# V of a head pair as 512-column products for three of five token chunks, in a fused mLSTM and retention step

## What is computed

```python
def retention_mixer(u, w_in, decay_exp, g_norm, w_out, S0, grid):
    z = jnp.einsum('btd,de->bte', u, w_in).astype(F32)
    hk, hv = B_HEADS * B_DK, B_HEADS * B_DV
    q, k, v, gate = jnp.split(z, [hk, 2 * hk, 2 * hk + hv], axis=-1)
    ...
    v = v.reshape(B, T, B_HEADS, B_DV).transpose(0, 2, 1, 3)
    ...
    h_f, S_f = retention_scan(q, k, v, log_gamma[0], S0[:, 0])
    h_b, S_b = retention_scan(flip_t(q), flip_t(k), flip_t(v), log_gamma[1], S0[:, 1])
```

## Time and profile before

| what | value |
|---|---|
| median of the runs | 2060.33 us (2056.77 to 2062.05, 3 runs) |
| the profiled execution | 2062.1 us, of which 2060.2 us is the span from the first to the last instruction |
| PE busy | 1940.7 us, 94% of the span |
| DVE, ACT, POOL busy | 1029.3, 712.1, 224.9 us |
| mean granted TensorE clock | 0.973 of full speed |

### The profile page before, as it was taken

How to read it: one execution, slowest core, us unless ns; L and a number is a source line. 1 busy time by engine, 2 the same in 40 slices (tenths; PEclk the granted TensorE clock), 3 DMA queues, 4 the chain that set the end, 5 groups by cost and what they waited for, 6 DMA issues and landing times.

```text
span 2060.2 us, 31485 instructions
## 1 busy us (share of the span) xinstructions
PE 1940.7 (94%) x12785; PEld 1825.5 (89%) x12785; DVE 1029.3 (50%) x1807; ACT 712.1 (35%) x912; POOL 224.9 (11%) x178
## 2 busy tenths in 40 slices
PE   7889999989999999997999999998997999999998
PEld 5668987759999999986999999997896999999997
DVE  4315435475653555566334343336376554355556
ACT  4314233344432333344322222224354443233333
POOL 3101001410000000240000001002240000000032
PEclk9989999999999999998999999999998999999999
DMA  9751302662213222344132231424742222322243
GB/s 286 276 181 32 113 27 72 241 219 62 74 52 100 79 64 71 108 128 150 47 97 61 67 97 36 126 74 162 248 123 59 64 66 64 94 82 63 64 138 113
DMA packets 273991, 220.34 MB, mean 107 GB/s; under 512 B 7995, under 2 KB 263731, under 8 KB 268275
## 3 DMA queue, kind: packets, MB, share of 16 engines
q1 hardware_dynamic: 262387, 196.33, 31.5%
q10 hardware_dynamic: 9808, 14.94, 2.5%
q0 software_dynamic: 1712, 7.88, 1.1%
HBM read 203.92 MB, written 11.01 MB: 104 GB/s over the span
## 4 chain that ended last, share of the span: by engine, by line
PE 80%; DVE 9%; ACT 3%; issue 3%; DMA 2%; POOL 2%; ACTq 1%; SPq 0%; DVEq 0%; POOLq 0%
PE PJ L1876 50%; PE PJ L1887 10%; PE PJ L2017 7%; PE AT L2185 1%; PE AT L1855 1%; PE AT L2169 1%; DVE uT L1212 1%; DMA hT<-in_ada_w 1%; DVE diag L1199 1%; PE AT L2182 1%; ACTq L916 1%; PE PJ L1901 1%; DVE uT L1227 1%; PE AT L2122 1%; ACT w_high L771 1%
## 5 line engine op out<-in xcount | busy, mean ns | idle before, releaser
L1876 PE MATMUL PJ<-h_both,w_high 128*128 128x320 f32 x4000 | 763.5, 313 | 14.6 <-DVE sq L1682 9.2
L1876 PEld LDWEIGHTS PJ<-h_both,w_high 128*128 128x128 f32 x4000 | 636.8, 190 | 18.7 <-issue 17.6
L1682 DVE SCALAR_TENSOR_TENSOR sq<-PJ,cols,sq 128x127 f32<-128x127 f32 x528 | 198.0, 430 | 261.7 <-ACT sq L1100 248.7
L1876 PE MATMUL PJ<-h_both,w_low 128*128 128x320 f32 x1344 | 307.8, 310 | 0.0
L550 POOL TENSOR_TENSOR sqsum<-sqsum,sq 128x320 f32<-128x320 f32 x60 | 116.7, 1944 | 1006.0 <-issue 821.6
L1876 PEld LDWEIGHTS PJ<-h_both,w_low 128*128 128x128 f32 x1344 | 225.9, 189 | 0.0
L760 ACT ACTIVATE w_high<-ring 128x2048 fp32r<-128x2048 f32 (+1 forms) x92 | 163.5, 1777 | 172.5 <-PE PJ L1876 103.2
L1275 DVE TENSOR_TENSOR w_low<-ring,w_high 128x2048 fp32r<-128x2048 f32 (+1 forms) x92 | 196.3, 2134 | 47.6 <-ACT w_high L760 47.6
L2017 PE MATMUL PJ<-w_high,h_both 128*128 128x256 f32 x960 | 179.6, 287 | 7.5 <-ACT xT L923 7.5
L2017 PEld LDWEIGHTS PJ<-w_high,h_both 128*128 128x128 f32 x960 | 153.0, 194 | 16.5 <-ACT xT L923 8.3
L1876 PE MATMUL PJ<-h_both,ring_low 128*128 128x320 f32 x656 | 152.2, 314 | 0.0
(11 more groups left out here) (267 smaller groups left out, 2870.1 us busy)
## 6 DMA issues: line engine op xcount, KB each, us to landing
ring<-in_ffn_w_up SPq DMA_DIRECT2D x88, 512.0 KB, 5.0
hT<-in_ada_w SPq DMA_DIRECT2D x30, 1024.0 KB, 4.9
ring<-in_ffn_w_down SPq DMA_DIRECT2D x64, 384.0 KB, 4.2
ring<-in_ret_w_in SPq DMA_DIRECT2D x24, 1024.0 KB, 6.5
ring<-in_ret_w_out SPq DMA_DIRECT2D x14, 1024.0 KB, 5.6
ring<-in_ml_w_in SPq DMA_DIRECT2D x12, 1024.0 KB, 9.5
turn<-in_ada_w SPq DMA_DIRECT2D x10, 1024.0 KB, 7.4
ring<-in_ffn_w_down SPq DMA_DIRECT2D x32, 320.0 KB, 3.6
```

What stands on the lines that cost most here:

```text
L1682: ins = v.scalar_tensor_tensor(o, z, scalar, o, ALU.mult, ALU.add)
L1876: ins = pe.matmul(PJ[:, s, b, 0:HALF], w[:, at + k * step:at + k * step + P], x[:, k, b * HALF:(b + 1) * HALF], start=(k == 0 and n == 0), ...
```

## The change

The two high buffers become the two halves of one tensor (`w_high_both`), and so do the low buffers of slots 2 and 3 (`low_both`), so that one moving operand of 512 columns can take 256 columns of the first head's weights and 256 of the second's. V of chunks 0 and 1 is still made per head with 256 columns, but V of chunks 2, 3 and 4 is made for both heads at once with 512 columns, one PSUM bank. The new order in a group is: chunks 0 and 1 of the first head, then chunks 2 to 4 of both heads, then chunks 0 and 1 of the second head (both in one PSUM slot). Ten tiles of 24 matmuls become four such tiles and three tiles of 24 matmuls of 512 columns; ACT's ten copies become six. The waits are renumbered accordingly.

```diff
-        w_high = [sb(f"w_high{s}", [P, UNIT], dt=F32R) for s in range(2)]
+        w_high_both = sb("w_high", [P, 2, UNIT], dt=F32R)
+        w_high = [w_high_both[:, s, :] for s in range(2)]
...
-            ring_low += [sb(f"ring_low{s}", [P, UNIT], stack, F32R) for s in pair]
+            low_both = sb(f"ring_low{pair[0]}", [P, 2, UNIT], stack, F32R)
+            ring_low += [low_both[:, s, :] for s in range(2)]
...
-                    load(3, w[0, :, ds(g * 512 + (2 * hk + 256), 256)], KT, 256, CH)
+                    load(3, w[0, :, ds(g * 512 + (2 * hk + 256), 256)], KT, 256, 1)
...
-                    for t in range(2 * CH):
-                        s = pj(2 + t // CH)
-                        a.activation(vt[:, t % CH, t // CH, 0:DV], PJ[:, s, 0, 0:DV], ACT.Copy).then_inc(pj_free[s], 1)
-                        if first and t == 3:
+                    for c in range(CH):
+                        s = pj(2)
+                        if c < 2:
+                            out, src = vt[:, c, 0, 0:DV], PJ[:, s, 0, 0:DV]
+                        else:
+                            out, src = vt[:, c, :, 0:DV], PJ[:, s, 0, :].rearrange("p (h v) -> p h v", h=2)
+                        a.activation(out, src, ACT.Copy).then_inc(pj_free[s], 1)
+                        if first and c == 2:
                             ada_row_out(P_EARLY[0])
-                        if t == CH - 1:
-                            high_unit(0, 2)
+                    high_unit(0, 2)
+                    s = pj(3)
+                    a.activation(vt[:, 0:2, 1, 0:DV], PJ[:, s, :, 0:DV], ACT.Copy).then_inc(pj_free[s], 1)
...
+                def value_tile(out, c, high, low):
+
+                    for k in range(KT):
+                        at = slice(k * DV, (k + 1) * DV)
+                        for n, (x, w) in enumerate(((u_high, high), (u_high, low), (u_low, high))):
+                            ins = pe.matmul(out, x[:, k, c * P:(c + 1) * P], w[:, :, at] if w is w_high_both or w is low_both else w[:, at],
+                                            start=(k == 0 and n == 0), stop=(k == KT - 1 and n == 2))
+                    return ins
+
                 def kv(after=None):
                     split_unit(1)
...
-                    for hh in range(2):
-                        split_unit(2 + hh)
-                        for c in range(CH):
-                            s = pj_slot()
-                            for k in range(KT):
-                                for n, (x, w) in enumerate(((u_high, w_high[hh]), (u_high, ring_low[2 + hh]),
-                                                            (u_low, w_high[hh]))):
-                                    ins = pe.matmul(PJ[:, s, 0, 0:DV], x[:, k, c * P:(c + 1) * P],
-                                                    w[:, k * DV:(k + 1) * DV], start=(k == 0 and n == 0),
-                                                    stop=(k == KT - 1 and n == 2))
-                            ins.then_inc(made[2 + hh], 1)
-                            if after:
-                                after(4 + hh * CH + c)
+                    split_unit(2)
+                    for c in range(2):
+                        s = pj_slot()
+                        value_tile(PJ[:, s, 0, 0:DV], c, w_high[0], ring_low[2]).then_inc(made[2], 1)
+                        if after:
+                            after(4 + c)
+                    split_unit(3)
+                    for c in range(2, CH):
+                        s = pj_slot()
+                        value_tile(PJ[:, s, 0, :], c, w_high_both, low_both).then_inc(made[2], 1)
+                        if after:
+                            after(2 + 2 * c)
+                            after(3 + 2 * c)
+                    s = pj_slot()
+                    for c in range(2):
+                        ins = value_tile(PJ[:, s, c, 0:DV], c, w_high[1], ring_low[3])
+                        if c == 1:
+                            ins.then_inc(made[3], 1)
+                        if after:
+                            after(12 + c)
```

More of the change, by code:

```diff
@@ L284, in hybrid_step @@
         EVACS_BEFORE_ML = 3
-        EVACS_BEFORE_RET = EVACS_BEFORE_ML + 9 * GROUPS[0] + (OUT0_FULL + 2 * OUT0_HALF + KT + DOWN_HALF) // 2 + FT
+        EVACS_BEFORE_RET = EVACS_BEFORE_ML + 7 * GROUPS[0] + (OUT0_FULL + 2 * OUT0_HALF + KT + DOWN_HALF) // 2 + FT
         PARTS = [(0, 0), (0, 16), (0, 32), (1, 0), (1, 16), (1, 32)]
@@ L489, in _ @@
                     sp.wait_ge(made[1], ffn_done)
-                    with loop(sp, GROUPS[layer] - 1, **per(4, 4, CH, CH)) as g:
+                    with loop(sp, GROUPS[layer] - 1, **per(4, 4, CH, 1)) as g:
                         load_v(g)
@@ L1035, in _ @@
                     ret_group(0, False, ret_tables)
-                    with loop(a, GROUPS[1] - 2, pjn=(pjn, 18), f0=(free[0], 9), f1=(free[1], 9), **per(4, 4, CH, CH),
+                    with loop(a, GROUPS[1] - 2, pjn=(pjn, 14), f0=(free[0], 7), f1=(free[1], 7), **per(4, 4, CH, 1),
                               gate=(gaten, 2), hd=(hd, 2), sc=(scn_h, 2), stg=(stg, 2),
@@ L1473, in _ @@
                         if hh == 0:
-                            pjn.add(18)
+                            pjn.add(14)
                             for s in range(SLOTS):
-                                outs[s].add((4, 4, CH, CH)[s])
+                                outs[s].add((4, 4, CH, 1)[s])
                             if h > 0:
@@ L1541, in _ @@
                         link(ins)
-                        head_tail(2 * h, hh, norm_col + 2 * h, EVACS_BEFORE_ML + 9 * (h // 2) + 8 + hh, False,
+                        head_tail(2 * h, hh, norm_col + 2 * h, EVACS_BEFORE_ML + 7 * (h // 2) + 6 + hh, False,
                                   hh if h < A_HEADS - 2 else None, range(2) if h == A_HEADS - 1 else ())
@@ L1606, in ret_group @@
                             link(ins)
-                            gcount.add(8 if hh == 0 else 1)
+                            gcount.add(6 if hh == 0 else 1)
                             head_tail(g * 4 + 2 * hh, hh, g * 4 + (norm_col + 2 * hh), gcount.now(), True,
@@ L1612, in _ @@
                     with loop(v, GROUPS[1] - 2, own=(own, 9), hd=(hd, 2), sc=(scnt, 2), dc=(dcnt, 2), oc=(ocnt, 2),
-                              gc=(gcount, 9), sw=(swn, 64), si=(sin_n, 64), so=(sout_n, 64), h0=(highs[0], 3),
+                              gc=(gcount, 7), sw=(swn, 64), si=(sin_n, 64), so=(sout_n, 64), h0=(highs[0], 3),
                               h1=(highs[1], 3)) as g:
@@ L1616, in _ @@
                     ret_group(GROUPS[1] - 1, True)
-                    pjn.add(18 * GROUPS[1])
+                    pjn.add(14 * GROUPS[1])
                     for s in range(SLOTS):
-                        outs[s].add(GROUPS[1] * (4, 4, CH, CH)[s])
+                        outs[s].add(GROUPS[1] * (4, 4, CH, 1)[s])
                 if layer == 0:
@@ L2194, in ret_group @@
                             turn_back()
-                    with loop(pe, GROUPS[1] - 1, pjn=(pjn, 18), f0=(free[0], 9), f1=(free[1], 9), h=(hrn, 2), sc=(scn, 2),
+                    with loop(pe, GROUPS[1] - 1, pjn=(pjn, 14), f0=(free[0], 7), f1=(free[1], 7), h=(hrn, 2), sc=(scn, 2),
                               st=(stc, 2), qz=(qzn, 4), hn=(hnn, 2), ro=(ron, 1), sp0=(splits[0], 3), sp1=(splits[1], 3),
```

## The result

The changed kernel takes 2074.85 us, the median of 5 runs (2071.29 to 2077.27), against 2061.99 for the kernel before, also over 5 runs (2056.77 to 2062.09). The ratio is 1.0068, interval 1.0053 to 1.0084: about 12.9 us slower. The forecast was 2066.0 in a range of 2060 to 2071, so the time lies above the range, on the side that had a chance of 0.41.

A forecast was written before the change was run, and what follows sets the result against it. PE's stream, busy 94% of the span, was taken to bound the kernel. Matmuls -5.8, stall +8.0, clock +4.3, lost saving +0.4 and layer 0 -1.5 gave +5.4 us: a median of 2066 us, range 2060 to 2071.

The forecast's parts named there:

- three signs of being wrong: Stall under 3 us, clock staying at 1.00 behind it in most groups, or a wide matmul not near 227 ns.
- The matmuls, -5.8 us: V products: 432 pairs of 256-column matmuls become 512-column ones of 226.7 ns, saving 13.3 ns a pair.
- the fixed part doesn't go away: Rival, chance 0.08: a wide V matmul takes 240 ns and saves nothing; 2071.5 us.
- The stall, +8.0: Layer 1, four groups: PE waits about 2.0 us longer each before the third V tile, for DVE's part of slot 3.
- The clock behind it: Layer 1: low clock follows the longer stall in three more groups, 1.44 us each, +4.3 us, between 0 and 6.0.
- 4.3 + 0.4 = 4.7: Layer 1: +4.3 us for the low clock behind stalls, +0.4 us for wide matmuls saving nothing at that clock.
- Layer 0: First group: conditioning steps paired behind wide tiles add -1.5 us, between -2.2 and +3; second group: no stall.
- Step 15: Conditioning product step in layer 0's first group: forecast to begin at 136.8, where it began at 140.02 before.
- -5.8 + 8.0 + 4.3 + 0.4 - 1.5 = +5.4 us: Whole kernel: matmuls, stall, clock behind it, saving lost at low clock, layer 0's first group; 2067.5 us for the profiled execution.
- C: Later theory: which later idle times the low clock follows hangs on when they come; changed kernel plus 0.88 us, 2067 to 2070.
- D: Later theory: wide products or new buffer places slow the rest themselves; changed kernel plus 0.88 us, 2075.7 us.
- That execution lies 1.8 us above the median of the three runs: Step from the profiled execution, 2062.1 us, to the median 2060.33: lowered the forecast from 2067.5 to 2065.7.

The follow-up runs named there:

- the two kernels with late issues: ACT's four transfer issues of layer 1 moved behind the second V tile's copy, in the changed kernel (2049.21 us) and in the kernel before (2054.29 us).
- the filled stall: Changed kernel with 25 useless 320-column matmuls on PE in the stall of each layer 1 group: 2069.36 us, ratio 1.0037.
- the second execution of the changed kernel: Changed kernel unaltered, run and traced again in the last session: median 2075.17 us, ratio 1.0054; the profiled execution took 2068.99 us.
- the three kernels with the 0.88 us shift: 6 useless matmuls behind V of layer 0's second group, added to the changed kernel (2071.26 us), to it with issues late (2045.25) and with stall filled (2065.68).
- wait alone: Kernel before, 256 columns kept, with PE's wait for the second head's weights moved ahead of the third V tile: 2072.92 us, ratio 1.0065.
- 2.5 us more: Kernel before with 17 useless 320-column matmuls ahead of the scores of layer 0's second group: 2069.55 us, ratio 1.0035.
- 3.4 us more: Kernel before with 23 useless 320-column matmuls ahead of the scores of layer 0's second group: 2066.71 us, ratio 1.0016.

## Why the prediction was wrong

None of the three signs of being wrong that it named came up: the stalls are 3.8 us and more, the clock is low behind all four, and a wide matmul takes 227 ns. Most of the miss lies where no sign looked.

*The matmuls, -5.8 us:* right. 0.94 us a group at full clock by the two kernels with late issues, 227 ns a matmul; -3.76 in layer 1. The Trainium skill ("TensorE: Matmul & The Clock Gate", section "Back-to-back issue gap") would have 512 / 2.4 + 2.5 = 215.8 ns for a wide one, by its rule for the gap of a matmul by itself; the rows disagree, as for the narrow one. The rival "the fixed part doesn't go away" is out.

*The stall, +8.0:* right in mechanism and size, +8.37.

*The clock behind it:* the mechanism is right; the filled stall shows it. The size, "12 x 0.120 = 1.44 us" a fall, was somewhat small. The first wide tiles take 8.11, 7.15, 7.16 and 7.16 us by the spacing of PE's starts, against 5.44. Three of them lose 1.7 us, near the forecast's 1.44 and 0.1 for the lost saving; the first loses 2.7, and its window of 4 us is the one that is at 0.50 throughout. In all four groups V of layer 1 holds 8.33 us over products and stalls, and before it held 2.48: +5.85 net, where 4.3 + 0.4 = 4.7 stood. It and the stall together account for +1.6.

*Layer 0:* V of both groups gained 2.85 us against 1.92 + 1.5 = 3.4. Step 15 began at 139.98, not near 137; a part of that is that the group began 1.7 us later, ahead of anything that the change touches. In five other traces with wide products it comes at 136.5 to 137.9, in the second execution of the changed kernel at 142.0: the forecast fits most of them. No stall in the second group, as forecast.

*The step that failed* is "**Sum.** -5.8 + 8.0 + 4.3 + 0.4 - 1.5 = +5.4 us on the profiled execution's 2062.1". It took every stage outside V as handed on unchanged, and counted the clock behind the four stalls only. By the traces those stages grew by 5.0 us: 1.7 ahead of the first V stage, 2.9 behind the last, the rest between. PE's idle time in them hardly moved, 108.3 us before and 107.4 after, but the time in which PE worked at the low clock there rose from 84.3 to 100.2 us. At 213 ns for 120 a microsecond at the low clock loses 0.44 us, so the 15.9 us more cost some 7.0 by this estimate, somewhat more than what was measured. Without them the sum would have come out at 2069.7, inside the range of 2060 to 2071.

With layer 0's V stages, that is for all but V of layer 1, the time at the low clock is 87.7 us before and 103.4 after, at an idle time of 109 to 113 us in every trace. In the three kernels with the 0.88 us shift and in the second execution of the changed one it is 84 to 92 us; in the two without the shift (stall filled, issues late) 116 and 102. With narrow products it is 83 (wait alone), 94 (issues late), 98 (2.5 us more) and 82 (3.4 us more). The 1.7 at the start is taken for one execution's luck: the first V stage begins at 88.8 to 90.7 in the traces with wide products and at 89.0 to 90.3 in those with narrow ones.

*What the runs say of its cause.* It stays open in part. C, the timing of the idle times, has four pairs of medians in the same direction: with 0.88 us of added work they are 3.6, 4.0 and 3.7 us lower in three kernels, and 3.4 us costs less than 2.5 in a fourth. Another rival, the session, was not tested: the first three pairs are each of two sessions, and the median of the kernel before moved from 2061.7 to 2064.6 us between sessions. The ratios to it, which take that out, move the same way, by 0.12 to 0.28%. D, as a fixed cost of the wide products, doesn't fit: it forecast 2075.7, 2050 and 2070 for the three kernels, and the second execution of the changed kernel spends 1859.1 us in the stages outside V, less than the 1861.1 before. That wide products raise this time on average by some other way isn't excluded. Nor is it settled what of the timing decides: two executions of the changed kernel differ by up to 10.8 us and two of the filled one with the shift by 19.5, with the clock share, and no run here tells in advance which idle time the low clock follows. C is supported, not shown, and the 5.0 us are those of one pair of executions.

*The last step, "That execution lies 1.8 us above the median of the three runs":* the median of more runs is 2061.7 to 2062.6 in three of four sessions and 2064.6 in one, so the profiled 2062.1 was no outlier. 1.5 of the error is this.

In all: 2067.5 + 1.6 (layer 1) + 0.6 (layer 0) + 5.0 (the rest) = 2074.7, where the profiled execution took 2074.81. Against the median that was forecast, 2066, the 1.5 comes on top.

## What to carry to other kernels

When an operand is merged so that a product needs two of its makers at once, ask what the second maker's engine does just before: here four transfer issues on ACT stood in the way of one copy, and the longer stalls with the clock behind them cost 14.2 us in layer 1 (8.37 + 5.85), where the products save 5.8 in all; with the issues moved the changed kernel comes to 0.9944 of the kernel before. Where PE is the bound, price a stall as its idle time plus what the clock costs behind it, here 1.7 to 2.7 us behind some 4 us. This kernel has many idle times of 2 to 3 us, and its time differs by 10 us and more between executions of one program: repeat such a kernel, read the clock of each run, and give a forecast under 0.5% a range that holds this.

## What was not expected of the hardware

An idle time of 2.28 us was followed by a granted 0.59 and one of 2.80 us at the same place by 1.00; with 0.88 us of work added ahead the medians were 3.6 to 4.0 us lower. Between executions of the changed kernel in one session the granted share ran from 0.965 to 0.972 and the time from 2077.52 to 2066.73 us. And the four issues on ACT take 4.25 us right behind the last K copy, but 3.25 us behind the second V tile's.
